# First picks for experts 0 and 1 alone, and two more experts scattered, in a two-layer mixture-of-experts trunk

## What is computed

```python
def hier_moe(h, router_group, router_expert, w_gate, w_up, w_down):
    # 32 experts in 4 groups; each token: best group, then its two best experts
    g_gate, g_idx = lax.top_k(softmax(xt @ router_group), 1)
    e_val, e_idx = lax.top_k(e_logits_of_that_group, 2)
    gate = g_gate * jax.nn.softmax(e_val, axis=-1)
    # for every expert e, over the tokens that chose it:
    #   y = (silu(x @ w_gate[e]) * (x @ w_up[e])) @ w_down[e]     (1024 -> 512 -> 1024)
    # token's result = sum over its two experts of gate * y

for layer in range(2):
    h = h + mixer(rms_norm(h))
    h = h + hier_moe(rms_norm(h), ...)
return rms_norm(h)
```

## Time and profile before

| what | value |
|---|---|
| median of 3 runs | 1605.1 us (1604.36 to 1606.85) |
| the profiled execution, its own time | 1607.02 us |
| its span, first to last instruction | 1605.3 us |
| mean granted TensorE clock | 0.994 |
| PE busy | 1548.7 us (96%) |
| DVE, ACT, POOL busy | 560.5, 347.3, 207.0 us |
| chain that ended last | PE 88%, DMA 7%, DVE 2%, issue 1% |
| mixture of experts, layer 0 | from about 261 to 744 us |
| mixture of experts, layer 1 | from about 1107 to the end |

### The profile page before, as it was taken

One profiled execution on the slowest core, in us unless ns is written; L12 is line 12 of the kernel. 1 busy time (PEld: TensorE's weight loads), 2 busy tenths in 40 slices (PEclk: granted clock), 3 DMA queues, 4 the chain that ended last, 5 costly groups with the idle time before them and its releaser, 6 DMA issues.

```text
span 1605.3 us, 22930 instructions
## 1 busy us (share of the span) xinstructions
PE 1548.7 (96%) x9576; PEld 747.5 (47%) x9576; DVE 560.5 (35%) x1305; ACT 347.3 (22%) x579; POOL 207.0 (13%) x252
## 2 busy tenths in 40 slices
PE   7999999999999999988999999999999999999977
PEld 4444545444444444424666666546444444444422
DVE  5222636232122222125344444436332122222125
ACT  3131621110000000013445454431010000000003
POOL 5000000000000000000344444420000000000000
PEclk9999999999999999999999999999999999999989
DMA  8711055999999999996411121133999999999994
GB/s 316 248 54 53 27 248 231 376 428 427 427 427 426 427 428 427 426 420 263 205 59 54 58 89 66 54 131 145 352 424 429 425 427 427 427 426 426 429 421 191
DMA packets 58492, 471.39 MB, mean 294 GB/s; under 512 B 12686, under 2 KB 12694, under 8 KB 30992
## 3 DMA queue, kind: packets, MB, share of 16 engines
q1 hardware_dynamic: 53760, 462.51, 69.7%
q0 software_dynamic: 4480, 7.29, 1.2%
q10 hardware_dynamic: 144, 0.05, 0.0%
HBM read 452.03 MB, written 23.35 MB: 296 GB/s over the span
## 4 chain that ended last, share of the span: by engine, by line
PE 88%; DMA 7%; DVE 2%; issue 1%; ACT 0%; SPq 0%; DVEq 0%
PE ps L814 25%; PE ps L650 16%; PE ps L829 12%; PE ps L1043 11%; PE ps L722 9%; PE ps L615 7%; DMA sb_ring<-in_w_up_dram 5%; DMA sb_ring<-in_w_down_dram 2%; PE ps L1061 2%; PE ps L966 2%; PE ps L820 1%; PE ps L738 1%; PE ps L749 1%; PE ps L599 1%; PE ps L764 1%
## 5 line engine op out<-in xcount | busy, mean ns | idle before, releaser
L814 PE MATMUL ps<-sb_ring,sb_work 128*56 128x512 f32 x2048 | 453.9, 595 | 20.5 <-issue 18.4
L814 PEld LDWEIGHTS ps<-sb_ring,sb_work 128*56 128x56 f32 x2048 | 147.8, 130 | 315.0 <-issue 314.6
L829 PE MATMUL ps<-sb_ring,sb_work 128*56 128x512 f32 x1024 | 231.0, 593 | 1.1 <-DMA sb_ring<-in_w_down_dram 1.1
L650 PE MATMUL ps<-sb_work,sb_h 128*64 128x224 f32 x2048 | 217.8, 356 | 0.0
L1841 DVE TENSOR_TENSOR sb_work<-sb_work,ps 56x512 f32<-56x512 f32 x64 | 69.4, 1085 | 347.1 <-ACT sb_work L1277 346.8
L1458 POOL DMA_INDIRECT expert_rows<-sb_work,sb_ri x56 | 51.1, 912 | 1068.7 <-DVE sb_work L1876 681.8
L650 PEld LDWEIGHTS ps<-sb_work,sb_h 128*64 128x64 f32 x2048 | 146.3, 137 | 67.0 <-issue 31.6
L1043 PE MATMUL ps<-sb_work,sb_ring 128*128 128x512 f32 x384 | 170.6, 598 | 1.1 <-DVE sb_work L1570 1.1
L1277 ACT ACTIVATE sb_work<-ps 56x512 f32<-56x512 f32 x64 | 37.7, 589 | 456.1 <-PE ps L814 456.1
L829 PEld LDWEIGHTS ps<-sb_ring,sb_work 128*56 128x56 f32 x1024 | 70.3, 130 | 120.8 <-issue 112.3
L1286 ACT ACTIVATE sb_work<-ps 56x512 f32<-56x512 f32 x56 | 33.1, 590 | 364.0 <-PE ps L829 364.0
(11 more groups left out here) (239 smaller groups left out, 1251.7 us busy)
## 6 DMA issues: line engine op xcount, KB each, us to landing
sb_ring<-in_w_down_dram SPq DMA_DIRECT2D x62, 2048.0 KB, 26.2
sb_ring<-in_w_gate_dram SPq DMA_DIRECT2D x56, 2048.0 KB, 23.3
sb_ring<-in_w_up_dram SPq DMA_DIRECT2D x56, 2048.0 KB, 27.4
sb_ring<-in_c_w_in_dram SPq DMA_DIRECT2D x8, 2048.0 KB, 8.6
sb_ring<-in_w_gate_dram SPq DMA_DIRECT2D x14, 1024.0 KB, 26.6
sb_ring<-in_w_up_dram SPq DMA_DIRECT2D x14, 1024.0 KB, 28.7
sb_ring<-in_ab_w_in_dram SPq DMA_DIRECT2D x5, 2048.0 KB, 11.1
expert_rows<-sb_work SPq DMA_DIRECT2D x2, 4096.0 KB, 20.6
```

What stands on the lines that cost most here:

```text
L650: mm = nc.tensor.matmul(dst[64 * z:64 * z + 64], a[:, 64 * z:64 * z + 64], b, start=start, stop=stop)
L814: mm = nc.tensor.matmul(dst[64 * z:64 * z + CAP, :], me["xgT"][:, j, c, q * CAP:(q + 1) * CAP], wblock(slots[z], NC)[:, c, :], start=(c == ...
L829: mm = nc.tensor.matmul(dst[64 * z:64 * z + CAP, :], src[:, c * CAP:(c + 1) * CAP], wblock(slots[2], FC)[:, c, z * 512:(z + 1) * 512], sta ...
```

## The change

It has two parts.

**At the start.** The first picks (`pick_first` on tiles 0 to 3) take the slots of experts 0 and 1 only, 112 columns instead of 224. The picks for experts 2 and 3, one for each token tile, stand between the first products: two inside experts 0 and 1, two behind them (`first_experts`). The picks of group 1 no longer stand in experts 0 and 1, so experts 2 and 3 do two banks each. Expert 5's gate and up are loaded in halves, the first when the first half of `gate_up` of expert 2 is read.

**At the end.** Experts 28 and 29 are scattered like the others (`NK` is 30), and only 30 and 31 are kept. There is one pair of late matrices instead of two: 4 transposes instead of 8 (moved behind the `gate_up` of expert 31), 8 matmuls of `late_add` instead of 16. For token tile 2 the first of the two rows read back is added by PE (`add_rows(l, NT - 2, (0,))`, 2 matmuls) instead of DVE. `rows_back` now waits for the scatters of 28 and 29 too. In layer 0 the transposed-tile copies on ACT stand behind all four squares, and the transposes use the banks that their own tile's sums used.

```diff
-PAIRS = LATE // 2
+NK = NE - 2
...
         def plan_norm(n):
...
-                    bk.add(("xt", n, t, half), (2 * t + half) % 8)
+                    bk.add(("xt", n, t, half), 2 * t + half if n == 0 else moe_bank(0, ADD_BANKS[t][half]))
...
# SP, moe_loads
                 piece(4, 4, 8)
                 for e in (3, 4):
                     wait_full(sp, ("dn", l, e - 3))
                     weight_load(l, e, 2)
-                for e in range(5, NS):
+                sp.wait_ge(gu_half, 4 * l + 4)
+                piece(5, 0, 4)
+                wait_full(sp, ("gu", l, 2))
+                piece(5, 4, 8)
+                wait_full(sp, ("dn", l, 2))
+                weight_load(l, 5, 2)
+                for e in range(6, NS):
...
# PE
+            def first_experts(l):
+
+                first_gate_up(l)
+                for e in range(2):
+                    turn(l, e)
+                    pick_first(l, e, part=1)
+                    out_rows(l, e)
+                pick_first(l, 2, part=1)
+                pick_first(l, 3, part=1)
+                slot_table(l)
...
+                if e == 3:
+                    pick(l, 1, 2, range(0, 8))
+                    turn(l, e)
+                    pick(l, 1, 3, range(0, 8))
+                    out_rows(l, e)
+                    return
+                b = 0 if e == 2 else q
+                pick(l, g + 1, b, range(0, 5))
+                turn(l, e)
+                pick(l, g + 1, b, range(5, 8))
+                out_rows(l, e)
+                if e == 2:
+                    pick(l, 1, 1, range(0, 8))
...
                 more_blocks(l)
-                late_turn(l)
-                late_add(l, 0, 0)
-                late_add(l, 0, 1)
                 last_gate_up(l, c, range(0, 4))
                 last_gate_up(l, c, range(4, 8))
                 last_gate_up(l, d, range(0, 4))
                 last_turn(l, c)
                 last_gate_up(l, d, range(4, 8))
+                late_turn(l)
                 last_down(l, c, range(0, 3))
                 last_turn(l, d)
                 last_down(l, c, range(3, 4))
                 last_down(l, d, range(0, 2))
                 last_down(l, d, range(2, 4))
-                late_add(l, 0, 2)
...
                 last_experts(l)
                 for t in range(NT - 1):
-                    late_add(l, 1, t)
-                late_add(l, 0, NT - 1)
-                late_add(l, 1, NT - 1)
-                add_rows(l, NT - 1)
+                    late_add(l, t)
+                add_rows(l, NT - 2, (0,))
+                late_add(l, NT - 1)
+                add_rows(l, NT - 1, (0, 1))
...
# ACT, norm_mid
                     square(2, t, h[:, t, :], junk2)
-                    if t == 1:
-                        take_turned(2, 0)
+                take_turned(2, 0)
                 take_turned(2, 1)
...
# POOL
-                for e in range(NS):
+                for e in range(NK):
                     wait_drained(pool, ("dn", l, e))
                     scatter_rows(l, e % 2, ri[:, e:e + 1]).then_inc(scattered[e % 2], 16)
...
# DVE
+            def take_first(l, b, part):
...
+                drains(v.tensor_tensor(me["xgT"][:, 0, 2 * b:2 * b + 2, part * n:(part + 1) * n],
+                                       bank(job)[:, 0:2 * n].rearrange("p (c s) -> p c s", c=2), g8, ALU.mult), job)
...
-                if e == 0:
+                if e == 1:
                     slot_lists(l)
-                if e == 1:
+                    for b in range(4):
+                        take_first(l, b, 1)
                     row_table(l)
+                if 2 <= e < NE - PICK:
+                    for b in {2: (0,), 3: (1, 2, 3)}.get(e, (q,)):
+                        take_pick(l, g + 1, b)
...
                 last_hidden(l, a)
                 last_turned(l, a)
-                dve.wait_ge(scattered[0], 16 * (l + 1) * (NS // 2))
-                late_selections(l).then_inc(late_ready, 1)
                 last_hidden(l, b)
                 last_turned(l, b)
-                dve.wait_ge(scattered[1], 16 * (l + 1) * (NS // 2))
-                keep_rows(l, a)
-                keep_rows(l, b)
+                out_rows(l, a)
+                out_rows(l, b)
                 more_blocks(l)
+                dve.wait_ge(scattered[0], 16 * (l + 1) * (NK // 2))
+                late_selections(l).then_inc(late_ready, 1)
...
                 combine(l, 1)
-                add_late(l, 0)
-                add_late(l, 1)
                 if l == 0:
+                    add_late(l, 0)
+                    add_late(l, 1)
                     norm_col(2, 0)
                     norm_rows(2, 0)
-                    combine(l, 2)
+                    combine(l, 2, (1,))
```

More of the change, by code:

```diff
@@ L300, in plan_moe @@
                     bk.add(("pick", l, g, b), moe_bank(l, b))
+                if g == 0:
+                    for b in range(4):
+                        bk.add(("second", l, b), moe_bank(l, b))
             for e in range(NE):
@@ L565, in _ @@
                 if i == 3:
-                    sp.wait_ge(h_ready, 2 * (NT - 1))
-                    wait_drained(sp, ("add", 0, NT - 1, 1))
+                    sp.wait_ge(h_ready, 2 * NT - 3)
+                    for t in (NT - 2, NT - 1):
+                        for nb in range(2):
+                            wait_drained(sp, ("add", 0, t, nb))
                     for part in range(3):
@@ L861, in expert @@
                 three = EXPERT_SLOTS[e % 3]
-                if e >= 2:
-                    for s, k in e_in[l * NE + e][0:2]:
-                        pe.wait_ge(ring_in[s], 16 * k)
-                    opens(("gu", l, e))
+                for s, k in e_in[l * NE + e][0:2]:
+                    pe.wait_ge(ring_in[s], 16 * k)
+                opens(("gu", l, e))
+                if e == 2:
+                    for b in range(4):
+                        wait_drained(pe, ("second", l, b))
+                    gate_up(l, three, g % 2, q, range(0, 4)).then_inc(gu_half, 1)
+                    fills(gate_up(l, three, g % 2, q, range(4, 8)), ("gu", l, e))
+                else:
                     if q == 0:
@@ L976, in add_rows @@
                 for nb in range(2):
-                    for k in range(2):
-                        mm = nc.tensor.matmul(bank(("add", l, t, nb))[:], diag[:, k, :],
-                                              yrow(t)[:, k, nb * 512:(nb + 1) * 512], start=False, stop=(k == 1))
+                    for k in ks:
+                        mm = nc.tensor.matmul(bank(("add", l, t, nb))[:], diag[:, k if t == NT - 1 else 2, :],
+                                              yrow(t)[:, k, nb * 512:(nb + 1) * 512], start=False, stop=(k == ks[-1]))
                     fills(mm, ("add", l, t, nb))
```

175 lines of the change are left out of this document (91 added, 84 removed).

## The result

The changed kernel takes 1595.35 us (median of 4 runs, 1594.12 to 1596.03), the kernel before 1605.97 in the same comparison; the ratio is 0.9932, with an interval of 0.9914 to 0.9949. It is 10.6 us faster, where 19.2 were forecast. The profiled execution has a span of 1593.6 against 1605.3, 11.7 us less.

What follows compares the result with a forecast made beforehand. It took the weight stream as the bound at each layer's end, with PE close behind and deciding layer 1's tail. Layer 0's 7.9 us plus layer 1's 11.3 gave 19.2, so 1605.1 became 1586; range 1580 to 1594.

Steps and rivals of the forecast that it cites:

- the likeliest case: Whole kernel: the forecast itself, 19.2 us faster at 1586 us, given a chance of 0.73.
- First product: Start of layer 0: first `gate_up` at about 272.3 instead of 276.82, 4.5 us earlier, with 49 ns per pick record.
- The stream behind the start: Weight loads from expert 7 on: land 5.2 us earlier in layer 0, 4.6 in layer 1, and the shift stays.
- the start gives nothing: Rival, start of both layers: loads of experts 6 and 7 come later, queue runs dry, 9.8 us go: 1596; chance 0.12.
- The full share of the middle of the layer: Middle of a layer's experts: DMA engines full at 427 GB/s, held against the rival of a start without gain.
- Scatters, late selections, read-back: Layer ends: added scatters cost 0.6 us in layer 0; waiting for scatters costs nothing; read-back keeps its place in the stream.
- The end, layer 0: End of layer 0: 3.3 us saved less 0.6 for scatters; with the stream's 5.2, 7.9 us earlier.
- ACT's order: End of layer 0: ACT no longer copies turned tile 0 ahead of the square of tile 2, 2.17 us.
- the 1.4 forecast: Late sums at the layer ends: the first now waits for ACT's two copies of expert 31's rows, 1.4 us lost.
- The rival of a clock that falls for a whole tail: Layer ends: new PE waits drop TensorE to 1.2 GHz, costing 47 us less 8 in one layer: 1625; chance 0.04.
- The end, layer 1: End of layer 1: 6.3 - 0.8 + 0.9 + 0.3 us saved; with the stream's 4.6, 11.3 us.
- the 6.3 us for L954 and L966: Layer 1, PE ahead of expert 30: L954 (1.65 us) and the sums L966 x8 (4.66) go, 6.3 us saved.

Runs made afterwards that it cites:

- the end alone: The changed kernel with the start of the kernel before, so only the change's second part is in; 1595.29 us, ratio 0.9923 to the kernel before.

## Why the prediction was wrong

The measured gain of 10.6 us lies outside the range, and the likeliest case was not what happened. By the profiled spans 19.2 us were forecast and 11.7 came.

- **First product: right.** 272.50 for 272.3, 49 ns for a record.
- **The stream behind the start: wrong, and this is the step that failed.** It is the passage from "finds the queue empty at best" over "So it lands 7.0 - 1.8 = 5.2 us earlier" to "so the shift stays". Expert 7's up block is issued at 342.91, as forecast (342.9):

```profile
sb_ring<-in_w_up_dram SPq DMA_DIRECT2D x1, 2048.0 KB, 13.1
```

It lands 13.1 us later and not 11.8, at 356.0, 3.9 us earlier than in the earlier trace rows. The shift then does not stay: the up block of expert 12 lands at 431.8 instead of 434.6, 2.8 us earlier, and that of expert 28 at 673.4 instead of 675.8, 2.4 us. The forecast took the landing of one block for the state of the stream. With a nearly empty queue the stream is not yet full behind this block either, which the 384 GB/s from 342.50 to 352.50 show, where 424 to 428 stood before. Counting what the stream misses from full shows the size of the loss: 3.2 us of 4.3 in layer 0, and in layer 1 4.0 of 4.4. Layer by layer it agrees only roughly with expert 28's start, by which 1.9 us are lost in layer 0 and 4.7 in layer 1; the two layers together make 7.2 and 6.6. In layer 1 the first product came 8.4 us earlier (1114.60 instead of 1122.97), expert 28 only 3.7 (1517.83 instead of 1521.50), which is 0.3 less than the 4.0 that layer 0 handed on; the forecast was 4.6 more. In the other executions with the new start, expert 28 starts 399.9 to 401.7 us after the first product in both layers, and 397.7 to 399.2 us in the kernel before and in the end alone, so about 2.5 to 3 of 4.4 us are lost as a rule, and this execution lost more in layer 1, with 403.2 us. This is the mechanism of the rival "the start gives nothing" (experts 2 and 3 carry two banks each, the requests for 6 and 7 come later relative to the first product, the queue runs dry), which was given 0.12, and its time, 1596, is nearly the one that was measured, in part by luck: it has no gain from the stream at all, where these profiles show 1.4 to 1.9 us a layer as a rule, and no term for the clock. The full share of the middle of the layer, which was held against it, says nothing on its first 80 us.
- **Scatters, late selections, read-back: right.** The late selections start at 706.75, 8.9 us behind the copy of expert 28's rows, held by its scatter for 4.8 us, and expert 30's product waits for ACT behind them, not for them.
- **The end, layer 0: right in size.** From expert 28 to the mixer's first product 3.3 us are gained (2.7 forecast). Some of it is the clock again: the kernel before had a fall in this stretch too (next point), where the changed kernel's comes behind it, in the mixer's product. ACT's order gives more than its term, 3.3 us in the run that takes it back. The wait of 1.35 us ahead of the late sums is the 1.4 forecast.
- **The clock: a cost that the sum lacked.** The rival of a clock that falls for a whole tail did not happen. But single falls of about 1.7 us came: one at the mixer's start cost layer 0 1.7 us, so that layer 1 began 4.0 us earlier, not 7.9. The forecast had argued from one wait of 3.00 us without a fall; a wait of 3.16 us at the same place now had one. The trace of before had one in the same layer, behind a wait of 3.19 us, which the forecast did not look at:

```profile
749.21 3.63 PE L599 MATMUL ps<-sb_ident,sb_ring 128*128 128x128 f32 x16 [3.19 <-DVE sb_ring L1561]
```

The changed kernel's first 16 transposes, at 740.83, take 1.91 us. The rule of the Trainium skill that was weighed there (TensorE: Matmul & The Clock Gate, HAM oscillation — how this bites in real kernels), that waits for transfers between bursts let the clock fall, was the better guide to where falls come: in 20 of 22 cases ahead of expert 29. The sum that the forecast tied to it, 1625, was not: a fall lasted a few us and not a whole tail.
- **The end, layer 1: more than forecast.** 8.0 us against 6.7 from expert 28 to the end. This is a sum of misses. The execution before waited 4.41 us ahead of expert 29, against 2.63 now and 3.00 in its layer 0, and its first 16 records took 5.99 us against 5.18: 2.6 us that the forecast did not count. It read that wait as PE's own, but expert 29's up weights landed then (issued at 1498.97, 33.9 us, so at 1532.9, and the product starts at 1533.00). Against this, of the 6.3 us for L954 and L966 about 1.7 were a slow clock, which did not go but moved to expert 30: 12.21 us for 48 records at 1547.25, where 10.52 stood before. The wait of 3.17 us that stood ahead of L954 is there still, now ahead of expert 30. And PE is no longer alone in deciding: expert 30's down weights, issued at 1531.27, land 32.6 us later, at 1563.9, and its `down` starts at 1563.95. So a shorter PE alone can gain nothing more there; the run without the branch, not measurably faster, fits that.

In sum, against the forecast: the stream 2.8 us short in layer 0 and 4.9 in layer 1, the clock 1.7, the ends 0.6 and 1.3 better, together 7.5 = 19.2 - 11.7. These are differences of two single executions. By the medians of the parts run alone the start gave nothing and the end 12 us, where 9.8 and 9.4 were forecast; how much of the end's surplus is the clock's was not taken apart.

## What to carry to other kernels

When a stream of transfers is the bound, count what it misses from full over the whole stretch, or follow the landings from block to block; one landing time tells of one block. A ring of n buffers can ask for block k + n only when block k is read, so starting earlier with the same work ahead of that point moves the hole and does not fill it. And a wait of PE can cost more than its length, through TensorE's clock: filling the waits with products that nobody reads gave 2.5, 2.2 and 1.3 us in the medians of three kernels, the first and the last against runs of another comparison. Look too at what a wait named "issue" ends with: here it was often the landing of a block.

## What the runs showed of the hardware

- A fall of the granted clock mostly costs 1.7 us of fp32 products (5.34 instead of 3.65 us for 16 records, 15.67 instead of 13.97 for 32), and 1.5 (5.18) to 2.9 us (6.59 for 16 records, in the profile with experts 5 to 9 in halves) at the ends of the range. It came behind waits of 2.0 to 4.4 us and not behind each of them: in the execution before, a wait of 3.00 us had none, and ahead of the mixer of layer 1 a wait of 2.0 us had one in four of eight profiles.
- The runs of one kernel differ in part by this. In the kernel with experts 5 to 9 in halves, the four runs at a clock of 0.996 or 0.997 took 1590.2 to 1592.4 us and the two at 0.991 and 0.992 1595.4 and 1595.8. It is not all: with the old start, halves and idle products the runs spread from 1592.3 to 1595.2 us at 0.996 to 0.998, and the slowest had the highest clock.
- PE stands still for 2.1 to 3.4 us behind the branch over the code for more than 56 tokens, in most executions: 0 and 3.17 us in the two layers before, 2.34 and 3.17 after. It goes with the branch. With idle products ahead in the program, and the branch in place, 701.50 and 1547.05 show waits of 0.74 and 1.28 us for weights alone. What decides whether it comes stays open.
